# Norm columns with the identity, a staged weight request, and gated expert rows on VectorE

## What is computed

```python
y = xf * lax.rsqrt(jnp.mean(xf * xf, axis=-1, keepdims=True) + RMS_EPS) * gain   # ln1, later final_g
proj = h @ w_in                                       # first product of the first block
ys = (silu(xb @ w_gate[e]) * (xb @ w_up[e])) @ w_down[e]    # for each block of routed tokens
out = zeros.at[buf_t].add(ys * buf_w[:, None])        # two experts' rows per token
x = x + g2 * out                                      # g2: one gate per column
return rms_norm(x, final_g)
```

## Time and profile before

| | us |
|---|---|
| median of 3 runs | 1887.66 |
| lowest and highest | 1886.74, 1889.07 |
| the profiled execution | 1889.26 |
| its span | 1887.9 |
| TensorE matmul busy (in the span) | 1721.7 |
| VectorE busy | 938.6 |
| ScalarE busy | 720.0 |
| POOL busy | 244.5 |

### The profile page before, as it was taken

The page is one execution under the profiler, slowest core; times in us unless marked ns, Lnnn a source line. Parts: engine busy times, 40 slices in busy tenths (PEclk is TensorE's granted clock), DMA queues, the critical chain, the costliest instruction groups (busy, mean ns, idle before and its releaser), DMA issues. The chain is left out here.

```text
span 1887.9 us, 24215 instructions
## 1 busy us (share of the span) xinstructions
PE 1721.7 (91%) x9178; PEld 1301.0 (69%) x9178; DVE 938.6 (50%) x1858; ACT 720.0 (38%) x1602; POOL 244.5 (13%) x225
## 2 busy tenths in 40 slices
PE   6999959988999999979999899998999948999991
PEld 5887749877888888868878677777888733333330
DVE  3743464454766665663425666653344762212224
ACT  3432762334333334543322367664334422212211
POOL 0000025101222210000000011110010113333320
PEclk9999979989999999989997799998999968999996
DMA  6221000042444443323200000005223338999953
GB/s 256 109 89 45 1 1 1 1 179 90 178 179 178 178 167 145 133 79 134 90 23 1 1 8 8 8 8 206 85 90 134 134 146 339 397 377 383 391 211 150
DMA packets 40081, 251.67 MB, mean 133 GB/s; under 512 B 17760, under 2 KB 17888, under 8 KB 23456
## 3 DMA queue, kind: packets, MB, share of 16 engines
q1 hardware_dynamic: 23120, 223.49, 30.2%
q10 hardware_dynamic: 3024, 15.07, 2.1%
q0 software_dynamic: 13824, 11.58, 1.9%
HBM read 293.99 MB, written 18.87 MB: 166 GB/s over the span
## 5 line engine op out<-in xcount | busy, mean ns | idle before, releaser
L600 ACT ACTIVATE units<-arena 128x512 fp32r<-128x512 f32 (+1 forms) x434 | 261.4, 626 | 489.4 <-PE banks L2211 484.7
L1187 DVE TENSOR_TENSOR units<-arena,units 128x512 fp32r<-128x512 f32 x388 | 263.7, 703 | 296.1 <-ACT units L600 295.7
L2209 PE MATMUL banks<-hx,units 128*128 128x512 f32 x800 | 315.8, 395 | 2.8 <-DVE arena L1638 1.7
L2210 PE MATMUL banks<-hx,units 128*128 128x512 f32 x800 | 312.9, 391 | 0.0
L2211 PE MATMUL banks<-hx,units 128*128 128x512 f32 x800 | 312.9, 391 | 0.0
L600 ACT ACTIVATE arena<-banks 128x512 f32<-128x512 f32 (+3 forms) x238 | 135.0, 571 | 266.8 <-PE banks L2146 100.4
L2146 PE MATMUL banks<-arena 128*128 128x128 f32 (+3 forms) x700 | 115.8, 300 | 66.5 <-ACT arena L600 16.8
L2209 PEld LDWEIGHTS banks<-hx,units 128*128 128x128 f32 x800 | 151.4, 189 | 34.6 <-issue 3.7
L2211 PEld LDWEIGHTS banks<-hx,units 128*128 128x128 f32 x800 | 151.2, 189 | 32.0
L2210 PEld LDWEIGHTS banks<-hx,units 128*128 128x128 f32 x800 | 151.3, 189 | 30.7
L2209 PE MATMUL banks<-units 128*128 128x512 f32 x416 | 165.1, 397 | 7.0 <-DVE units L1187 7.0
(11 more groups left out here) (413 smaller groups left out, 2500.3 us busy)
## 6 DMA issues: line engine op xcount, KB each, us to landing
arena<-in_moe_gu SPq DMA_DIRECT2D x32, 2048.0 KB, 9.6
arena<-in_w_in SPq DMA_DIRECT2D x17, 2048.0 KB, 9.2
arena<-in_moe_dn SPq DMA_DIRECT2D x32, 1024.0 KB, 9.0
arena<-in_ada SPq DMA_DIRECT2D x12, 2048.0 KB, 10.5
arena<-in_w_gu SPq DMA_DIRECT2D x11, 2048.0 KB, 7.9
arena<-in_w_out SPq DMA_DIRECT2D x4, 2048.0 KB, 7.8
arena<-in_w_down SPq DMA_DIRECT2D x4, 2048.0 KB, 9.2
arena<-in_cmp_w SPq DMA_DIRECT2D x2, 2048.0 KB, 8.1
```

The costliest lines, as they stand in the source:

```text
L600: return func(dst, src, ACT.Copy, scale=scale)
L1187: tt(U[:, u % 4, 1, :], src, U[:, u % 4, 0, :].bitcast(F32), SUB).then_inc(*up("gemm_dve", "lo", c.part, u))
L2209: pe.matmul(bs[i], sh[:, q], mh, start=c.first and k == 0, stop=False)
L2210: pe.matmul(bs[i], sh[:, q], ml, start=False, stop=False)
```

## The change

It has six edits. The first 80 of the per-partition columns are requested right behind the identity, under a signal of their own, and the others behind the first product; the waits follow. SP waits for `w_in0` to land before it requests `w_in1`. VectorE evicts both halves of each expert block, as products with the gate row, and the gate leaves the final tiles, where weight, row sum and x go into one instruction. ScalarE loads the root's table after the last expert block. Tile 0 is multiplied by the final gain while ScalarE squares the last tile, and ScalarE multiplies it by its root and signals the store.

```diff
--- before.py
+++ after.py
@@ -821,25 +821,26 @@
     ones1 = m.ones[:, 0:1]
     x_v = I["x"].rearrange("(t p) d -> p t d", p=128)
     a.dma_start(m.cst[:, 0:256], I["consts"][:, 0:256]).then_inc(*up("dma_id", by=16))
+    a.dma_start(m.col[:, 0:80], I["cols"][:, 0:80]).then_inc(*up("dma_ln", by=16))
 
     a.wait_ge(*at("norm_dve", "pads"))
     func(m.rs_tmp[:, 63:64], m.cpad[0][:, 0:1], ACT.Sqrt)
     for t in (0, 2):
         a.wait_ge(*at(f"x_in{t}"))
         func(m.junk0[t // 2], m.x0[:, t, :], ACT.Square, accum_out=m.ss[:, t:t + 1]).then_inc(*up("norm_act", "sq", "ln1", t))
-        if t == 0:
-            a.dma_start(m.col, I["cols"]).then_inc(*up("dma_col", by=16))
     root("ln1", m.r4, m.rs_tmp[:, 0:4])
-    a.wait_ge(*at("dma_col"))
+    a.wait_ge(*at("dma_ln"))
 
     def hx_hi(f):
         a.wait_ge(*at("norm_pe", "xt", "ln1", f))
         copy(m.hx["in"][:, 0, f, :], s.bank("hx", "ln1", f), C["ln1"][:, f:f + 1]).then_inc(*up("norm_act", "hi", "ln1", f))
     first_gemm("w_in0", "ln1", m.x0, m.x0, m.r4, hx_hi, 0)
+    a.dma_start(m.col[:, 80:], I["cols"][:, 80:]).then_inc(*up("dma_col", by=16))
     a.dma_start(m.cst[:, 256:], I["consts"][:, 256:]).then_inc(*up("dma_cst", by=16))
     for c, name in enumerate(WIN):
         if c:
             gemm(name, WIN[c - 1])
+    a.wait_ge(*at("dma_col"))
     narrow("wba", 8, C["wba"], "in")
     for i in range(4):
         item("w_in6", i)
@@ -1079,12 +1080,6 @@
                        bias=m.mod[:, 24 + f:25 + f], scale=m.sc2[:, f:f + 1])
         ins.then_inc(*up("moe_act", key, i))
 
-    def rows_out(key, i, n):
-        a.wait_ge(*at("moe_pe", key, i, 0))
-        if n >= 4:
-            a.wait_ge(*at(f"yo{n % 4}", n - 4))
-        copy(m.yo[n % 4][:, 0:512], s.bank("moe", key, i, 0)).then_inc(*up("moe_act", "yo", n))
-
     def more_hidden(d):
         a.wait_ge(*at("moe_pe", "aTd", d))
         if d:
@@ -1110,12 +1105,9 @@
             tokens("xT", m.xT[(i + 1) % 2], i + 1)
             if i % 2:
                 tokens("xTd", m.xTd, d + 1)
-        rows_out("dn", i, out_of(i))
-        if i % 2 == 0 and i:
-            rows_out("dnd", d - 1, more_of(d - 1))
     more_hidden(NPAIR // 2 - 1)
-    rows_out("dnd", NPAIR // 2 - 1, NBLK - 1)
-
+
+    func(m.rs_tmp[:, 63:64], ones1, ACT.Sqrt)
     a.wait_ge(*at("moe_pe", "gu", NPAIR - 2))
     a.dma_start(m.fg, I["fg"]).then_inc(*up("dma_fg", by=16))
     yr = m.y_d.rearrange("(t p k) d -> t p (k d)", p=128, k=2)
@@ -1130,6 +1122,9 @@
             a.wait_ge(*at("norm_act", "sq", "fg", t - 1))
         func(m.att[:, 0, :], m.x4[:, t, :], ACT.Square, accum_out=m.ss[:, t:t + 1]).then_inc(*up("norm_act", "sq", "fg", t))
     root("fg", m.r4, m.rs_tmp[:, 0:4])
+    a.wait_ge(*at("norm_dve", "rstd", "fg"))
+    a.wait_ge(*at("fin_dve", "fg"))
+    copy(m.x4[:, 0, :], m.x4[:, 0, :], m.r4[:, 0:1]).then_inc(*up("fin_act", "out", 0))
 
 def dve_program(nc, m, s, p):
     v, at, up = nc.vector, s.at, s.up
@@ -1482,7 +1477,7 @@
     v.wait_ge(*at("norm_act", "sq", "ln1", 2))
     rstd("ln1", m.r4, m.ss, 1024.0)
     scale_halves("ln1", m.x0, m.x0, m.r4)
-    v.wait_ge(*at("dma_col"))
+    v.wait_ge(*at("dma_ln"))
     first_lo("w_in0", "ln1", "in", C["ln1"], 0)
     v.wait_ge(*at("norm_dve", "pads"))
     for c, name in enumerate(WIN):
@@ -1493,6 +1488,7 @@
                 swa_table(2 * c - 6 + k // 6)
         if c:
             gemm(name, WIN[c - 1], between)
+    v.wait_ge(*at("dma_col"))
     narrow("wba", 8, C["wba"], "in", m.ba_tmp)
     v.wait_ge(*at("gemm_pe", "rows", "wba"))
     v.tensor_copy(m.bb[:, 0:32], s.bank("rows", "wba")[:, 0:32]).then_inc(*up("gemm_dve", "rows", "wba"))
@@ -1843,13 +1839,17 @@
         ins.then_inc(*up("moe_dve", key, i))
 
     def rows_out(key, i, n):
-        v.wait_ge(*at("moe_pe", key, i, 1))
-        if n >= 4:
-            v.wait_ge(*at(f"yo{n % 4}", n - 4))
-        v.tensor_copy(m.yo[n % 4][:, 512:1024], s.bank("moe", key, i, 1)).then_inc(*up("moe_dve", "yo", n))
+
+        for half in range(2):
+            q = slice(512 * half, 512 * half + 512)
+            v.wait_ge(*at("moe_pe", key, i, half))
+            if n >= 4 and half == 0:
+                v.wait_ge(*at(f"yo{n % 4}", n - 4))
+            tt(m.yo[n % 4][:, q], s.bank("moe", key, i, half), m.grow[:, q], MUL).then_inc(*up("moe_dve", "yo", n, half))
 
     tokens("xT", m.xT[0], 0)
     tokens("xTd", m.xTd, 0)
+    v.wait_ge(*at("row_act", "g2", 1))
     for i in range(NPAIR):
         d = i // 2
         v.wait_ge(*at("moe_act", "silu", i))
@@ -1876,12 +1876,13 @@
         y1, y2 = m.ring[t][:, 0:1024], m.ring[t][:, 1024:2048]
         v.wait_ge(*at(f"y_in{t}"))
         ch(stt(y1, y2, R(4)[:, t:t + 1], y1, MUL, ADD))
-        ch(stt(y1, y1, R(5)[:, t:t + 1], m.grow, MUL, MUL))
-        ch(tt(m.x4[:, t, :], m.x4[:, t, :], y1, ADD), "x", t)
+        ch(stt(m.x4[:, t, :], y1, R(5)[:, t:t + 1], m.x4[:, t, :], MUL, ADD), "x", t)
+    v.wait_ge(*at("dma_fg"))
+    v.wait_ge(*at("norm_act", "sq", "fg", 0))
+    ch(tt(m.x4[:, 0, :], m.x4[:, 0, :], m.fg, MUL), "fg")
     v.wait_ge(*at("norm_act", "sq", "fg", 3))
     rstd("fg", m.r4, m.ss, 1024.0)
-    v.wait_ge(*at("dma_fg"))
-    for t in range(4):
+    for t in range(1, 4):
         stt(m.x4[:, t, :], m.x4[:, t, :], m.r4[:, t:t + 1], m.fg, MUL, MUL).then_inc(*up("fin_dve", "out", t))
 
 def dve_route(v, m, s):
@@ -2085,8 +2086,7 @@
                              oob_is_err=False).then_inc(*up(sem, key, by=16))
 
     def scatter(block, n):
-        g.wait_ge(*at("moe_act", "yo", n))
-        g.wait_ge(*at("moe_dve", "yo", n))
+        g.wait_ge(*at("moe_dve", "yo", n, 1))
         g.indirect_dma_start(out=m.y_d, out_offset=off(m.idx[:, 0, block:block + 1]), in_=m.yo[n % 4], in_offset=None,
                              bounds_check=1023, oob_is_err=False).then_inc(*up(f"yo{n % 4}", n, by=16))
 
@@ -2646,7 +2646,7 @@
     def down(key, aT, w, i, n_out):
         wd = [ap.rearrange("p (k n) -> p k n", k=2) for ap in w]
         for n in range(2):
-            b = take(("moe", key, i, n), (("moe_act", "moe_dve")[n], "yo", n_out))
+            b = take(("moe", key, i, n), ("moe_dve", "yo", n_out, n))
             for k in range(2):
                 for half, rows in enumerate(H64):
                     ins = pe.matmul(b[rows, :], aT[:, k, rows], wd[half][:, k, n * 512:(n + 1) * 512], start=k == 0,
@@ -2769,6 +2769,8 @@
             fence(16)
             before.clear()
         load(name)
+        if name == "w_in0":
+            sp.wait_ge(*at("ring0", "w_in0"))
         if name.startswith("moe"):
             e = int(name[3:])
             if e == 3:
@@ -2782,7 +2784,7 @@
                 down(e)
     o = out.rearrange("(t p) d -> t p d", p=128)
     for t in range(4):
-        sp.wait_ge(*at("fin_dve", "out", t))
+        sp.wait_ge(*at("fin_dve" if t else "fin_act", "out", t))
         sp.dma_start(o[t], m.x4[:, t, :]).then_inc(*up("dma_out", t, by=16))
     sp.wait_ge(*at("dma_out", 3))
```

## The result

| | median of n runs, us | ratio to the kernel before, 95% interval |
|---|---|---|
| kernel before, beside the changed one | 1888.37 (8) | |
| changed kernel, first set | 1882.26 (8) | 0.9966, 0.9951 to 0.9981 |
| changed kernel, four more sets (r1_after, r2_after, r3_after, r5_after) | 1881.13 (6), 1879.64 (9), 1881.41 (6), 1879.87 (5) | 0.9962, 0.9965, 0.9959, 0.9950 |

The changed kernel is faster, by 6.1 us in the first set and by 8.1 in the median of all its 34 runs (1880.66) beside 149 of the kernel before (1888.74). That is 0.3 to 0.5%: small, but no interval reaches 1. The forecast was 1877.4 with a range up to 1880.6: the first set lies above it, the median of all runs at its upper edge. The profiled execution took 1884.53 us, span 1883.2, against 1889.26 and 1887.9.

A forecast was written before the change was run, and what follows sets the result against it. TensorE, busy nine tenths of the span, was taken to bound the middle, so only edits at the two ends could show. Their terms summed to -10.3 us, from a median of 1887.66 to 1877.4, range 1875.0 to 1880.6.

The forecast's parts named there:

- Front end: Start of the kernel: ScalarE's scaling starts with the statistics, about 11.3 instead of 15.36 us, for -4.1 us.
- small transfer: Front end: the 40 KB of norm columns beside x cost 0.1 to 0.35 us; net taken as zero, ±0.4.
- first weight chunk: Front end: lands at about 13.4 us instead of 15.1, 1.7 us gained, before ScalarE wants it at 14.45.
- Clock ramp: First products: TensorE's rise from 1.2 to 2.4 GHz moves with the start; first 0.39 us matmul near 21.
- Expert stage: Middle: VectorE's 24 added evictions fit into its idle time, cost zero; bounds 0 and 16.6 us.
- Final tiles: Back end: two instructions instead of three, 2.64 instead of 3.90 us a tile, -5.0 us if y is there.
- Root: Back end: with its table loaded earlier, the root starts at about 1877.2 instead of 1878.21, -1.0 us.
- final gain: Back end: tile 0's early product costs at most +0.05 us; an earlier first store request gives -0.2, between 0 and -1.2.
- stores: End of the kernel: only an earlier first request helps; last store comes 7.1 us after it.
- rival 3: Back end: stores follow VectorE, the last request counts, not the first; -11.3 us, 1876.4; chance 0.05.
- The sum: Whole kernel: -4.1 - 5.0 - 1.0 + 0.05 - 0.2 = -10.3 us, giving 1877.4 from the median of 1887.66.
- rival 1: TensorE's clock does not follow: rise not earlier, or a later stage falls at another moment; -8.3 us, 1879.4; chance 0.15.

The follow-up runs named there:

- r4_unstaged: Changed kernel without the synchronous queue's wait between weight chunks 0 and 1, second set: 1882.19 us, ratio 0.9965.
- r2_late: Changed kernel without SP's wait, its 40 KB of norm columns requested behind ScalarE's first square, where all columns were before: 1882.02 us, ratio 0.9963.
- back edits alone: Changed kernel with the two front-end edits put back as before, two sets: 1885.21 and 1883.29 us, ratios 0.9978 and 0.9975.

## Why the prediction was right or wrong

**Front end: right in its mechanism and size.** -4.1 forecast; -3.6 in the first pair, -4.1 between the means of the eight starts with the old front end (17.2 us) and the ten with the new (13.1). x's last square began at 8.96 where the first profile of the kernel before had 8.54, so scaling starts at 11.76, not 11.3. That lies within the scatter, and no run shows it to be the price of the small transfer: the square begins at 8.53 to 9.17 with the old front end and at 8.72 to 9.00 with the new. The first weight chunk landed by 13.85 (13.4 forecast, 14.4 the limit). SP's wait is not what brought it forward, since r4_unstaged does without it and the first chunk landed 11.2 us after its request at 2.72, at 13.9:

```profile
DMA to landing us min/median/max: 11.2/11.2/11.2
```

That leaves the columns that no longer run beside it, as forecast, with 1.2 us gained instead of 1.7. For the columns' own lateness, size was the wrong reason, as r2_late shows.

**Clock ramp: right.** The first matmul of 0.39 us came at 20.69, 7.4 us after the start, forecast near 21; it was 8 before.

**Expert stage: right.** VectorE's product takes 693 ns, the copy took 693, and its idle time before these instructions is still 45.6 us for 48.

**Final tiles: right but for y.** 2.64 us a tile, and no wait for y inside the loop. But the first tile began 5.56 us after the request instead of 4.86: 0.7 us later, more than the bound "-5.0 and, with y half a microsecond late, -4.5" allowed. The landing of y itself took 5.2 to 5.5 us in every profile with both new ends, 4.7 to 4.9 in all others. Why, no run tells.

**Root, final gain, stores: right.** -1.0 for the root, which starts 0.20 us after the mean's start instead of 1.20. The mean still came 1.29 us after the last sum. The first request for a store came 1.18 us after the first final product instead of 1.32, -0.14 (forecast -0.2), and the span ended 7.1 us after it, as before, though the fourth request came 2.53 instead of 3.58 us behind the first. One us of the stores in the changed kernel, columns as in rows 8 with each engine's busy time:

```profile
1878.00:1879.00 1.00, 0.00 (x0) 0.00 (x0) 0.60 (x1) 0.00 (x0) 0.00 (x0) 0.50 1.00 393
```

The DMA engines are busy all through it, and the end kept its distance from the first request, not from the last: rival 3 is out.

**The sum: the step that failed is that the middle stays as it is.** The sum has no term for it. -10.3 was set against ends that gave -9.2 in the first pair and -9.7 on average, so the terms that it has were right to 0.6 us on average. "I take this ramp to move with the start" dealt with the first rise of the clock only, and with it I held the clock question closed, though the profiles show TensorE for 167 to 195 us of each execution at the lower level later on, a different time from one execution to the next. This is the second half of rival 1, "a later stage falls to the lower level at another moment", to which I gave 0.15 and 2.05 us. In the first pair of profiles the middle gave back 4.5 us, with 194.6 us at the lower level in place of 174.1, and 4.4 of it in the stretch near 1000 us, where the granted clock is 0.63 in place of 0.78. Over 34 runs it is 2.2 us (9.7 less 7.5), of which the clock explains a part: in the runs of the changed kernel the time rises by about 1.2 us for 0.001 less clock (five at 0.941 average 1885.4, seven at 0.946 1879.3), and some 0.0011 of clock are missing (0.0015 looked for, 0.0004 found). That would be 1.3 us, an estimate beside the 1.7 ± 1.5 from the profiles. The rest, and the 1.6 us that the back edits alone lack, stay open, and so does why the clock is lower.

**The base.** 1877.4 was measured from a median of three runs, 1887.66; 149 runs give 1888.74, and 1.1 us of the miss is that. Of the 3.3 us by which the changed kernel's 34 runs lie above the forecast (1880.66), 1.1 are the base, 0.6 the ends, and 1.6 the middle (2.2 when means are taken instead of medians); the first set lay another 1.6 higher, which is chance. The range had terms for every edit and none for this: single executions of either kernel spread with a standard deviation of 2 to 3 us, so a median of three or eight is itself uncertain by a microsecond or more. Its lower side was not worked out either: the bounds of the terms reach 1876.0, not 1875.4.

## What to carry to other kernels

Work at the two ends could be summed from rows here to within 0.6 us on average; what the middle does with it could not, since TensorE's granted clock changes within a run and not alike in each. Measure the middle (first to last matmul) apart from the ends in several profiles of the same kernel before one pair is read as cause and effect, and put its scatter into the range. A small transfer that gates the start is best requested ahead of the big streams; here the time of its request counted for more than its size.

## What the runs showed of the hardware

- 40 KB of columns, requested at 4.7 us behind x and 2 MB weight chunks on another queue, landed after 9.7 and 10.2 us; requested 3.5 us sooner, after 5.1 to 5.5. The 685.5 KB took 10.7 to 11.5.
- The same program, busy on the same matmuls with no transfer running, was granted 0.50 throughout 989 to 994 us in one execution and 0.69 in another. A stretch of some 30 us took 4 us longer with it. Over nineteen profiles of ten kernels the middle grew by 0.27 us for each us more at 0.50.
- With both ends shortened, the first of four transfers of 1 MB took 0.4 to 0.7 us longer to land than in the kernel before (5.2 to 5.5 us beside 4.8), from a request at the same distance (4.4 us) behind the start of the last matmul.
